# Where TensorE waits for the split of an exchanged activation chunk: at the next unit's first matmul, or in front of the matmuls that read it

## The reference

```
x = x + rms_norm( (concat(mla(h), fox(h)) * silu(gates)) @ w_out ) ; h = rms_norm(x)       # first block
x = x + 0.5 * swiglu(rms_norm(x))                  # ffn1, inner width 5632
x = x + hybrid_mixer(rms_norm(x))                  # three dilated attentions, a spatial gate, w_out_2
x = x + 0.5 * swiglu(rms_norm(x))                  # ffn2
out = rms_norm(x)
```

## Time and profile before

| | us |
|---|---|
| median of 3 runs | 2650.59 (2650.52 to 2651.16) |
| the profiled execution, its own time | 2646.32 |
| its span (first to last instruction) | 2644.5 |
| PE busy | 2611.7 |
| DVE busy | 1494.1 |
| ACT busy | 1186.9 |

### The profile page before, as it was taken

How to read it: one execution, slowest core, us unless ns; L and a number is a source line. 1 busy time by engine, 2 the same in 40 slices (tenths; PEclk the granted TensorE clock), 3 DMA queues, 4 the chain that set the end, 5 groups by cost and what they waited for, 6 DMA issues and landing times.

```text
span 2644.5 us, 32030 instructions
## 1 busy us (share of the span) xinstructions
PE 2611.7 (99%) x11785; PEld 2167.5 (82%) x11785; DVE 1494.1 (56%) x1700; ACT 1186.9 (45%) x1349; POOL 174.8 (7%) x292
## 2 busy tenths in 40 slices
PE   9999999999999999999999999999999999999998
PEld 8888778788888888888888888888788888888886
DVE  7755665755555555556655665555655555555554
ACT  5544553444444444444444554444444444444333
POOL 0110000000000000001100310000100000000000
PEclk9999999999999999999999999999999999999999
DMA  7876656577777776667876576665777777777554
GB/s 216 261 223 197 210 181 192 159 223 212 221 213 221 217 216 212 209 209 256 244 216 185 157 213 211 206 206 189 225 206 207 222 212 222 213 220 227 193 190 151
DMA packets 277138, 552.87 MB, mean 209 GB/s; under 512 B 21978, under 2 KB 24888, under 8 KB 276792
## 3 DMA queue, kind: packets, MB, share of 16 engines
q1 hardware_dynamic: 257520, 489.88, 60.7%
q0 software_dynamic: 19024, 61.54, 7.9%
q10 hardware_dynamic: 504, 0.26, 0.0%
HBM read 521.70 MB, written 29.89 MB: 209 GB/s over the span
## 4 chain that ended last, share of the span: by engine, by line
PE 98%; DVE 1%; issue 1%; ACT 0%; DMA 0%; SPq 0%; DVEq 0%; ACTq 0%
PE acc L547 95%; PE s_ps L675 1%; PE tr L587 1%; PE o_ps L698 1%; DMA raw<-in_w_in 0%; PE tr L903 0%; DVE act_lo L1380 0%; DVE merged_lo L1405 0%; DVE stats L1440 0%; DVE xres L1848 0%; ACT merged_hi L1019 0%; ACT whi L962 0%; DVE wlo L1348 0%; DVE xres L1838 0%; DVE xres L1567 0%
## 5 line engine op out<-in xcount | busy, mean ns | idle before, releaser
L1348 DVE TENSOR_TENSOR wlo<-raw,whi 128x1024 fp32r<-128x1024 f32 x929 | 1130.8, 1223 | 1003.8 <-ACT whi L962 1000.1
L962 ACT ACTIVATE whi<-raw 128x1024 fp32r<-128x1024 f32 x929 | 978.6, 1057 | 1174.2 <-PE acc L547 1158.4
L547 PE MATMUL acc<-whi,act_hi 128*128 128x512 f32 (+1 forms) x2560 | 692.7, 392 | 8.3 <-issue 7.0
L547 PE MATMUL acc<-whi,act_lo 128*128 128x512 f32 (+1 forms) x2560 | 682.9, 389 | 0.0
L547 PE MATMUL acc<-wlo,act_hi 128*128 128x512 f32 (+1 forms) x2560 | 682.7, 388 | 0.0
L547 PEld LDWEIGHTS acc<-whi,act_lo 128*128 128x128 f32 x2560 | 479.7, 188 | 100.1
L547 PEld LDWEIGHTS acc<-wlo,act_hi 128*128 128x128 f32 x2560 | 479.8, 188 | 99.6
L547 PEld LDWEIGHTS acc<-whi,act_hi 128*128 128x128 f32 x2560 | 473.3, 188 | 101.7 <-issue 9.3
L547 PE MATMUL acc<-wlo,h_hi 128*128 128x512 f32 x704 | 188.4, 389 | 0.0
L547 PE MATMUL acc<-whi,h_lo 128*128 128x512 f32 x704 | 188.4, 389 | 0.0
L547 PE MATMUL acc<-whi,h_hi 128*128 128x512 f32 x704 | 188.4, 389 | 0.0
(11 more groups left out here) (257 smaller groups left out, 1364.6 us busy)
## 6 DMA issues: line engine op xcount, KB each, us to landing
raw<-in_w_in SPq DMA_DIRECT2D x280, 512.0 KB, 4.4
raw<-in_ffn_w_gate SPq DMA_DIRECT2D x176, 512.0 KB, 4.4
raw<-in_ffn_w_up SPq DMA_DIRECT2D x176, 512.0 KB, 3.9
raw<-in_ffn_w_down SPq DMA_DIRECT2D x176, 512.0 KB, 4.6
raw<-in_w_out SPq DMA_DIRECT2D x64, 512.0 KB, 4.7
turn_dram<-h_turned POOLq DMA_DIRECT2D x25, 512.0 KB, 3.2
h_back<-turn_dram POOLq DMA_DIRECT2D x100, 128.0 KB, 5.6
raw<-in_w_sg_out SPq DMA_DIRECT2D x24, 512.0 KB, 3.8
```

The lines of the kernel that those rows point to most:

```text
L547: return nc.tensor.matmul(pair[:, half, 0:width], left[:, k, half * P:(half + 1) * P], right[:, slot, t, 0:width], start=start, stop=stop, ...
L962: nc.scalar.activation(whi[:, slot, :, 0:width], raw[:, slot, :, 0:width], ACT.Copy).then_inc(hi_ready, 1)
L1348: nc.vector.tensor_tensor(wlo[:, slot, :, 0:width], raw[:, slot, :, 0:width], whi[:, slot, :, 0:width].bitcast(F32), ALU.subtract).then_in ...
```

## The change

Only PE's program is edited. After it, a unit's first matmul no longer counts the chunks that it doesn't read: `exchanged` is called later. In the gate units nothing is counted until the end of the fourth (two chunks at once); the third chunk is counted, and waited for by an explicit `chunk_is_split()`, after group 3 of the first w_out unit, in front of PE's transposes of the fourth chunk and of the groups 4 and 5 that read the third. The w_out_2 units and ffn2's first unit get the same. In merge chunks 1 to 3 the count moves from GA's j = 6 to GS's j = 6, so that the spatial-out unit has the wait in place of the attention-out unit. The number of chunks counted is the same at the end.

```
                     attention_at(n)
                     n += 1
-                    if c and j == 7:
-                        exchanged()
+                    if (c, j) == (3, 7):
+                        exchanged(CHUNKS - 2)
 
             for c in range(CHUNKS):
                 for j in groups(G_D, o_hi, o_lo):
                     if c == 0 and j == 0:
                         attention_at(n)
                     if c == 0 and j == 3:
+                        exchanged()
+                        chunk_is_split()
                         transpose_chunk(o_sb, 3 * W)
...
                     if not first_one and j == 3:
+                        exchanged()
+                        chunk_is_split()
                         transpose_chunk(xres, 3 * W)
...
                     if first_one:
                         if 1 <= j <= 6:
                             spatial(j - 1)
-                    if j == 6:
-                        exchanged()
+                        if j == 6:
+                            exchanged()
                 for j in groups(2, att_hi, att_lo):
                     pass
                 for j in groups(G_D, act_hi, act_lo):
-                    if first_one and j == 6:
-                        exchanged(SG_W // W)
+                    if j == 6:
+                        exchanged(SG_W // W if first_one else 1)
...
                     if j == 3:
                         if c == 0:
                             transpose_chunk(mixed)
-                        else:
-                            exchanged()
+                        elif c == CHUNKS - 1:
+                            exchanged(CHUNKS - 2)
```

## The result

| | before | after |
|---|---|---|
| median | 2650.88 (4 runs, 2650.52 to 2651.42) | 2628.10 (4 runs, 2627.62 to 2629.78) |
| profiled execution | 2646.32 | 2629.78 |
| its span | 2644.5 | 2628.0 |

The ratio is 0.9915 (95% interval 0.9898 to 0.9932): 22.8 us less, where 17.0 was forecast. A second comparison on one chip gave 0.9921 (0.9907 to 0.9935): 2627.47 against 2648.49, 21.0 us. The profiled executions differ by 16.5 us, close to the forecast. So two things are to be explained: why that pair agrees with the sum, and why the timed runs gained some 4 to 6 us more.

What follows compares the result with a forecast made beforehand. PE bounds the kernel, so time is gained only where it stands still or runs at the lower clock. Gate 4.3, first w_out 4.1, merge 2.9 and w_out_2 with ffn2 5.7 sum to 17.0: 2650.59 to 2633.6 us, range 2630 to 2638.

Steps and rivals of the forecast that it cites:

- rival E: At the nine places the wait is another semaphore than chunk_split and stays: 2650.6 us, 4%.
- the cover: Time from the third chunk's split to PE's transposes: 9.3 us in w_out, 9.2 in ffn2; explicit waits cost nothing meanwhile.
- The two new waits: In gate units 2 and 3 PE would wait 0.41 us each on ACT's softmax, near 332.6 and 358.6 us.
- the lead: In gate units 2 and 3 PE starts 2.54 us sooner and keeps all but 0.41: 4.3 us for both.
- rival C: ACT and DVE make gate units 2 and 3 lose all 4.3 us: gain 12.7, time 2637.9 us, 7%.
- rival F: New explicit waits before the fourth chunk's transposes in w_out and ffn2 bite: slower by 0.2% (5.3 us), 2%.
- Each removed wait is worth its length: At all nine places the gain is the wait's length, less what PE then waits for next.
- I take 1.58: First w_out unit: the clock drop goes with the wait, worth 1.58 us, bounds 0 and 1.58.
- the only stretch below 1.00: Ground for the 1.58 us: from 20 to 2640 us only the clock behind the first w_out unit's wait is below 1.00.
- Rival D: More clock drops in the timed runs, at the other two gate waits: gain 20.2, time 2630.4 us, 8%.
- the 4.27 us: The median of the runs shown lies 4.27 us above the profiled execution, for no reason that a row shows.
- B: The clock drop stays or moves to another short PE wait, or was absent: gain 15.4, time 2635.2 us, 15%.

Runs made afterwards that it cites:

- e9: The changed kernel with heads 4 and 6's transposes of the probabilities and values one group later on all engines: 0.9917 of the kernel before, median 2627.00 us.
- e1: The kernel before, unchanged, timed and profiled once more: median 2649.22 us (11 runs), profiled execution 2648.64.
- e3: The kernel before with only the merge edit: ratio 0.9982 to the kernel before, 4.5 us less.
- e4: The kernel before with only the w_out_2 and ffn2 edits: ratio 0.9972 to the kernel before, 6.9 us less by the medians.
- e7: The changed kernel with the third gate wait put back and no explicit wait in w_out: 0.9934 of the kernel before, median 2631.01 us.
- e2: The kernel before with only the gate and first w_out edits: ratio 0.9961 to the kernel before, 9.5 us less by the medians.
- e6: The kernel before with ten small matmuls in each of the three gate waits, every wait kept: ratio 0.9992, 1.7 us less by the medians.

## Why the prediction was wrong, point by point

- **Which wait, and where it goes: right.** All nine waits were `chunk_split`, all nine are gone (rival E is out), and the cover worked out for each kind of place held. The two new waits are 0.45 and 0.39 us where 0.41 was forecast, and e9 shows that they are the softmax. With their restarts they took back 1.3 us, and no more of the lead was given back in the gate units (rival C is out). The explicit waits cost nothing (rival F is out).
- **"Each removed wait is worth its length": this step failed.** A wait costs its length in the profile and about 0.3 us more. From start to start 3 x 2.54 were worth 8.3 us instead of 7.6, 3 x 0.97 were worth 3.8 instead of 2.9, and 3 x 1.90 were worth 6.5 instead of 5.7. Less the same for the two new waits this is about 2 us. The overlap could have been read ahead of the run, in 1.07 us bars that start every 0.91.
- **"I take 1.58" for the clock: the second step that failed.** It was sized from one execution that had one drop, and was carried over to the median of other executions. In the traces with gate waits (the first profile, e1, e3, e4, e7) 7 of 13 waits of 2.54 us have a drop behind them, and 2 of 15 of the waits of 1.90 (the first profile, e1, e2, e3, e6). For three waits of each kind that is 2.0 drops or 3.2 us in a mean run, not 1.58; with so few waits counted this is an estimate. The ground that I gave, "the only stretch below 1.00", was weak besides: in a window of 2255 us one such drop changes the mean by less than 0.001 and can't be seen. It takes windows of some 10 us at each wait, or the chain's pieces.
- **The sum again.** Idle 16.2, restarts 9 x 0.27 = 2.4, new waits -1.2, drops 3.2: 20.6 us. Measured were 21.0 (17.2 to 24.6 by the interval) and 22.8 (18.0 to 27.0). The first profiled pair: 16.2 + 2.4 - 1.2 + 1.6 for its one drop - 1.6 for the drop at the start of after = 17.4, less 0.85 for its later first weights (9.92 against 9.07) = 16.5; 16.5 were measured. Its agreement with the 17.0 on record is luck: the 2 us of hidden cost that the sum left out, and the 2.4 us that this one execution of the changed kernel lost at its start, cancel.
- **Rival D was right in its direction** as to the clock, and the 4.27 us between the profile and the runs shown were the sign of it. Its size was not: it put a drop on all three gate waits of every timed execution, where no trace with three has more than two, and it had none behind the waits of 1.90 us, where e3 and e6 have one each. I had it at 8% and let the range end 0.4 us below it. With the restarts, which no case had, its 2630.4 becomes 2628.4; that this is near the 2628.1 measured is in part luck, since its three drops are one too many. The page "TensorE: Matmul & The Clock Gate" of the Trainium skill (section "Part 1: The HAM clock gate") says that the monitor runs freely; the traces agree, in that the same wait at the same place has a drop in one execution and not in the next. It spoke for D as much as for B, and I drew only B from it.
- **Do the timed executions have these drops?** They have no trace, but their mean granted clock is on record. By the windows above a drop is 12 x (1 - 0.86) x 2 = 3.4 us at half the clock, so it lowers the mean over a span of 2645 us by 0.0006 and costs 1.6 us, that is 2.5 us for 0.001. The 58 later executions of before are 6 at 0.998 (mean 2646.6 us), 47 at 0.997 (2649.0) and 5 at 0.996 (2651.8): steps of 2.4 and 2.8 us. None of the nine profiles with one drop or none stands below 0.998. So most of the 52 at 0.997 or lower had two drops or more, wherever these lay, which bears out the 2.0 and speaks against the one drop of the sum on record. The rounding to 0.001 leaves the exact mean open.
- **Open.** The four runs of before in the first comparison (2650.5 to 2651.4) lie above most of the 58 later ones, whose medians by job and kernel are 2648.5 to 2649.2. For them no clock is on record, so whether they had more drops or a slower start stays open, and with it 1.8 of the 22.8 us.

## What to carry to other kernels

Measure a wait from start to start in the stream, not as the idle time of pipelined bars: here a wait of PE cost 0.24 to 0.31 us more than was drawn, and one of 1.2 us cost 1.5. A wait that a later consumer needs should stand in front of that consumer: nine waits moved gave 0.8%, although PE was drawn 99% busy. And before a profile's own time is carried to a median, see whether it is typical: if the runs differ from it by more than the effect's uncertainty, the terms that vary from run to run are sized by several profiles, not one.

## What the runs showed of the hardware that I had not expected

- A half-clock stretch (1.2 GHz) came behind 7 of 13 waits of 2.54 us and 15 of 40 waits of 2.48 us, 2 of 15 of 1.90 us, and none of 40 of 1.22 us, 15 of 0.97 to 1.30 us, or 13 of 1.7 us (in front of ffn1, one in each profile). Each cost 1.6 us.
- Waits of one length at even distances had it behind mostly every third, so the drops aren't independent from wait to wait. That they depend on where the wait falls in time would fit this; no run here moved the waits alone to show it.
